# Prompt attention on one core: a head's score products in one run, then its value products

## The reference

```
o_c = softmax(q   . ck^T / 8, causal over 32 compressed blocks) . cv
o_s = softmax(q_r . ks^T / 8, causal) . vs
o_w = softmax(q_r . kw^T / 8, causal) . vw
o   = gate0 * o_c + gate1 * o_s + gate2 * o_w
```

## Time and profile before

| | us |
|---|---|
| median of 3 runs | 2354.88 |
| the profiled execution | 2356.08 |
| its span, first to last instruction | 2354.3 |
| TensorE busy with matmuls | 2059.4 (87%) |
| VectorE, ScalarE, POOL busy | 924.4, 610.2, 133.2 |
| mean granted TensorE clock | 0.838 |

### The profile page before, as it was taken

One profiled execution on the slowest core, in us unless ns is written; L12 is line 12 of the kernel. 1 busy time (PEld: TensorE's weight loads), 2 busy tenths in 40 slices (PEclk: granted clock), 3 DMA queues, 4 the chain that ended last, 5 costly groups with the idle time before them and its releaser, 6 DMA issues.

```text
span 2354.3 us, 33541 instructions
## 1 busy us (share of the span) xinstructions
PE 2059.4 (87%) x13375; PEld 1838.6 (78%) x13375; DVE 924.4 (39%) x1372; ACT 610.2 (26%) x847; POOL 133.2 (6%) x171
## 2 busy tenths in 40 slices
PE   3999676999999696997687779999998699999968
PEld 3777375999999696996574447777788699999958
DVE  4687745433334644114011122322333634343363
ACT  4222144322312223221101111222123423232223
POOL 0000003000000000004000021011100200000000
PEclk8999797999999898996666655555589799999979
DMA  4211013322222121213221200000003122222211
GB/s 131 59 36 36 18 54 118 97 83 89 89 89 89 36 77 53 72 54 92 55 62 46 72 0 1 1 1 1 1 1 99 36 90 87 91 82 79 89 36 56
DMA packets 149763, 138.82 MB, mean 59 GB/s; under 512 B 22674, under 2 KB 146914, under 8 KB 149471
## 3 DMA queue, kind: packets, MB, share of 16 engines
q1 hardware_dynamic: 148175, 129.94, 17.8%
q0 software_dynamic: 1504, 7.74, 1.0%
HBM read 130.79 MB, written 10.87 MB: 60 GB/s over the span
## 4 chain that ended last, share of the span: by engine, by line
PE 82%; DVE 9%; issue 2%; ACT 2%; SPq 1%; POOL 1%; DMA 0%; ACTq 0%; DVEq 0%; POOLq 0%
PE ps L360 47%; PE ps L1209 5%; PE ps L439 3%; PE ps L1182 3%; PE ps L399 3%; PE ps L1180 2%; PE ps L1196 2%; PE ps L1194 2%; PE ps L913 1%; DVE sub_out L1899 1%; PE ps L1052 1%; PE ps L739 1%; PE ps L738 1%; PE ps L740 1%; DVE rstd L466 1%
## 5 line engine op out<-in xcount | busy, mean ns | idle before, releaser
L360 PE MATMUL ps<-x_hi,w_hi 128*128 128x272 f32 x1920 | 409.4, 295 | 75.7 <-DVE x_lo L481 33.9
L360 PE MATMUL ps<-x_hi,w_lo 128*128 128x272 f32 x1920 | 404.1, 293 | 0.0
L360 PE MATMUL ps<-x_lo,w_hi 128*128 128x272 f32 x1920 | 403.2, 292 | 0.0
L360 PEld LDWEIGHTS ps<-x_hi,w_hi 128*128 128x128 f32 x1920 | 308.4, 193 | 84.4 <-issue 47.8
L345 DVE TENSOR_TENSOR w_lo<-w_raw,w_hi 128x2048 fp32r<-128x2048 f32 x102 | 233.6, 2293 | 250.1 <-ACT w_hi L340 249.1
L360 PEld LDWEIGHTS ps<-x_lo,w_hi 128*128 128x128 f32 x1920 | 309.3, 193 | 0.0
L360 PEld LDWEIGHTS ps<-x_hi,w_lo 128*128 128x128 f32 x1920 | 307.0, 193 | 0.0
L340 ACT ACTIVATE w_hi<-w_raw 128x2048 fp32r<-128x2048 f32 x102 | 194.5, 1907 | 296.5 <-PE ps L360 287.6
L360 PE MATMUL ps<-hid_hi,w_lo 128*128 128x272 f32 x1024 | 212.0, 288 | 0.0
L360 PE MATMUL ps<-hid_hi,w_hi 128*128 128x272 f32 x1024 | 211.6, 288 | 0.0
L360 PE MATMUL ps<-hid_lo,w_hi 128*128 128x272 f32 x1024 | 211.1, 288 | 0.0
(11 more groups left out here) (339 smaller groups left out, 2838.9 us busy)
## 6 DMA issues: line engine op xcount, KB each, us to landing
w_raw<-in_ffn_w_in SPq DMA_DIRECT2D x64, 512.0 KB, 4.6
w_raw<-in_ffn_w_out SPq DMA_DIRECT2D x64, 512.0 KB, 4.3
w_raw<-in_nsa_w_in SPq DMA_DIRECT2D x20, 512.0 KB, 4.3
w_raw<-in_conv_w_in SPq DMA_DIRECT2D x16, 512.0 KB, 5.5
w_raw<-in_ple_w_gate SPq DMA_DIRECT2D x16, 512.0 KB, 4.2
w_raw<-in_conv_w_out SPq DMA_DIRECT2D x8, 512.0 KB, 4.4
w_raw<-in_nsa_w_o SPq DMA_DIRECT2D x8, 512.0 KB, 4.6
x_tok<-in_x_prompt SPq DMA_DIRECT2D x4, 512.0 KB, 8.1
```

The lines of the kernel that those rows point to most:

```text
L360: m = pe.matmul(o_, w[par][:, wcols:wcols + P], x[:, k, c_], start=f, stop=l)
```

## The change

TensorE's step i now makes the row scores of head i + 1 and the transposed scores of head i, fill by fill in turn, with nothing between them; then, of the same head i, ten value products of the selected branch, the shift transposes, and the ten of the window branch. The compressed branch and the output transposes stand between scores and values. The loop is one step shorter, PT has one head instead of two. In a tile the correction product comes second and the mask last, and the correction of `score_rows` has 68 rows too, for which POOL clears the four rows of QB ahead of each head. ScalarE's and VectorE's lists follow. POOL's first keys, queries (of two heads now), compressed values and values are made before `end_phase` 8, behind its work for the samples, with a wait for the stores of the caches, since the buffer of the values (VX) now lies over part of their source; ScalarE's rounded copies for them stand at the start of its work for the samples.

```diff
-        (PT,), e = over(xt_at, ("pT", [P, 2, 5, SEQ], F32))
+        (PT,), e = over(xt_at, ("pT", [P, 5, SEQ], F32))
...
+        (VX,), e = over(kv_at, ("v_one", [P, 2, 2, QT, HD + 1], F32))
+        assert e <= kv_at + size([P, 2, NTT, 256]), e - kv_at
...
         def samp_act(act, L):
+            keys_high(act, L, 0)
+            for i in range(2):
+                q_high(act, L, i)
...
-        STEPS = range(-1, NHD + 1)
+        STEPS = range(-1, NHD)
...
                     pe.matmul(out, qa[:, qs], KA[g % 2][:, br, 0:n], start=True, stop=False)
-                    pe.matmul(out[:, qt * P:n], IDB[:, :], CAUB[:, :], start=False, stop=False)
-                    m = pe.matmul(out, qb[0:HD, qs], KB[g % 2][0:HD, br, 0:n], start=False, stop=True)
+                    pe.matmul(out, qb[0:HD + 4, qs], KB[g % 2][0:HD + 4, br, 0:n], start=False, stop=False)
+                    m = pe.matmul(out[:, qt * P:n], IDB[:, :], CAUB[:, :], start=False, stop=True)
                 m.then_inc(S["s_full"], 1)
...
                     pe.matmul(out, KA[g % 2][:, br, ks], qa[:, kt * P:SEQ], start=True, stop=False)
-                    pe.matmul(out[:, 0:P], CAUB[:, :], IDB[:, :], start=False, stop=False)
-                    m = pe.matmul(out, KB[g % 2][0:HD + 4, br, ks], qb[0:HD + 4, kt * P:SEQ], start=False, stop=True)
+                    pe.matmul(out, KB[g % 2][0:HD + 4, br, ks], qb[0:HD + 4, kt * P:SEQ], start=False, stop=False)
+                    m = pe.matmul(out[:, 0:P], CAUB[:, :], IDB[:, :], start=False, stop=True)
                 m.then_inc(S["t_full"], 1)
 
-            def values(i, br, j):
+            def values(i, br):
                 g = i // GQ
-                if j == 0:
-                    pe.wait_ge(S["t_exp"], 5 * i + (3, 5)[br])
-                    if i:
-                        pe.wait_ge(S[("a_free", "b_free")[br]], i)
-                    if i % GQ == 0:
-                        pe.wait_ge(S["v_prep"], 2 * (g + 1))
-                for qt, kt in V_ORDER[2 * j:2 * j + 2]:
+                pe.wait_ge(S["t_exp"], 5 * i + (3, 5)[br])
+                if i:
+                    pe.wait_ge(S[("a_free", "b_free")[br]], i)
+                if i % GQ == 0:
+                    pe.wait_ge(S["v_prep"], 2 * (g + 1))
+                for qt, kt in V_ORDER:
                     slot, c = p_tile(br, kt, qt)
-                    m = pe.matmul(PS[:, 4 + br, qt * (HD + 1):(qt + 1) * (HD + 1)], PT[:, i % 2, slot, c:c + P],
+                    m = pe.matmul(PS[:, 4 + br, qt * (HD + 1):(qt + 1) * (HD + 1)], PT[:, slot, c:c + P],
                                   VX[:, g % 2, br, kt, :], start=kt == 0, stop=kt == qt)
-                if j == 4:
-                    m.then_inc(S[("a_full", "b_full")[br]], 1)
...
                 for j in range(5):
                     if i + 1 < NHD:
                         score_rows(i + 1, j)
-                    if i >= 1:
-                        values(i - 1, 0, j)
+                    if i >= 0:
+                        score_cols(i, j)
+                if i % 2 == 0 and i >= 2:
+                    out_rows(i // 2 - 1)
                 if (i + 1) % GQ == 0 and i + 1 < NHD:
                     cmp_scores((i + 1) // GQ)
-                if i % GQ == 0 and 0 <= i < NHD:
+                if i % GQ == 0:
                     cmp_probs(i // GQ)
-                for j in range(5):
-                    if 0 <= i < NHD:
-                        score_cols(i, j)
-                    if i >= 1:
-                        values(i - 1, 1, j)
-                    if j == 2 and i + 1 < NHD:
-                        shift(i + 1)
-                if i % GQ == 0 and 0 <= i < NHD:
+                if i >= 0:
+                    values(i, 0)
+                if i + 1 < NHD:
+                    shift(i + 1)
+                if i % GQ == 0:
                     cmp_out(i // GQ)
-                if i % 2 and i >= 3:
-                    out_rows((i - 3) // 2)
+                if i >= 0:
+                    values(i, 1)
...
             def exps(i, j):
                 act.wait_ge(S["t_full"], 5 * i + j + 1)
-                if i >= 2 and j == 0:
-                    act.wait_ge(S["b_full"], i - 1)
-                L(act.activation(PT[:, i % 2, j, :], PS[:, 2 + (5 * i + j) % 2, :], ACT.Exp), S["t_exp"], wait=False)
+                if i and j == 0:
+                    act.wait_ge(S["b_full"], i)
+                L(act.activation(PT[:, j, :], PS[:, 2 + (5 * i + j) % 2, :], ACT.Exp), S["t_exp"], wait=False)
...
-                if i + 2 < NHD:
-                    q_high(i + 2)
-                if i % GQ == 0 and 0 <= i < NHD:
+                    keys_high(act, L, i // GQ + 1)
+                if 2 <= i + 2 < NHD:
+                    q_high(act, L, i + 2)
+                for j in range(5):
+                    if i >= 0:
+                        exps(i, j)
+                if i % 2 == 0 and i >= 2:
+                    out_rows(i // 2 - 1)
+                if i % GQ == 0:
                     cmp_probs(i // GQ)
-                for j in range(5):
-                    if 0 <= i < NHD:
-                        exps(i, j)
-                    if j == 2 and i + 1 < NHD:
-                        shift_rows(i + 1)
+                if i + 1 < NHD:
+                    shift_rows(i + 1)
+                if i % GQ == 0:
+                    cmp_out(i // GQ)
                 if (i + 1) % GQ == 0 and i + 1 < NHD:
                     cmp_exp((i + 1) // GQ)
...
-                if i >= 2:
-                    combine_win(i - 2)
-                if i % GQ == 0 and 0 <= i < NHD:
-                    cmp_norm(i // GQ)
+                if i >= 1:
+                    combine_win(i - 1)
                 if i + 1 < NHD:
                     for j in range(5):
                         maxima(i + 1, j)
                     shift(i + 1)
                 if (i + 1) % GQ == 0 and i + 1 < NHD:
                     cmp_max((i + 1) // GQ)
-                if i >= 1:
-                    combine_sel(i - 1)
+                if i >= 0:
+                    combine_sel(i)
+                if (i + 1) % GQ == 0 and i + 1 < NHD:
+                    cmp_norm((i + 1) // GQ)
             combine_win(NHD - 1)
...
+            L(pool.memset(QB[i % 3][HD:HD + 4, :].bitcast(F32), 0.0))
+            L(pool.tensor_copy(QA[i % 3][other, :], hi), S["q_prep"])
+            L(pool.tensor_tensor(QB[i % 3][0:HD, :], QR[rows, i // 2, 0:SEQ], hi, ALU.subtract), S["q_prep"])
...
+            keys(pool, L, 0)
+            queries(pool, L, 0)
+            queries(pool, L, 1)
+            cmp_vals(pool, L, 0)
+            pool.wait_ge(stores, 16 * N_KV_ST)
+            L(pool.memset(VX[:, :, :, :, HD:HD + 1], 1.0))
+            vals(pool, L, 0)
+
...
             samp_pool(pool, L)
+            prompt_prep(pool, L)
             end_phase(pool, 8)
```

More of the change, by code:

```diff
@@ L244, in trunk @@
         (ON, OU), _ = over(p_at, ("o_tok", [P, 2, QT, P], F32), ("o_win", [P, QT, HD], F32))
-        (OCS, PPC, PCT, VX, ATS, MXT, NMB_), e = over(
+        (OCS, PPC, PCT, ATS, MXT, NMB_), e = over(
             t_at, ("o_cmp", [P, QT, GQ, HD], F32), ("p_c", [P, QT, GQ, 32], F32), ("p_cT", [P, SEQ], F32),
-            ("v_one", [P, 2, 2, QT, HD + 1], F32), ("att_small", [P, 96], F32), ("max_cols", [P, 2, QT, 4], F32),
+            ("att_small", [P, 96], F32), ("max_cols", [P, 2, QT, 4], F32),
             ("max_bf", [P, 8], BF16))
         assert e <= t_at + 6 * 2176, e - t_at
+        (VX,), e = over(kv_at, ("v_one", [P, 2, 2, QT, HD + 1], F32))
+        assert e <= kv_at + size([P, 2, NTT, 256]), e - kv_at
         (YTOK,), e = over(f_at, ("y_tok", [P, NTT, D], F32))
@@ L1058, in samp_pe, with keys_high, q_high @@
                 pe.wait_ge(S["ots_ready"], t + 1)
+        def keys_high(act, L, g):
+            if g >= 2:
+                act.wait_ge(S["t_full"], 5 * GQ * (g - 1))
+            for br in range(2):
+                L(act.activation(KA[g % 2][0:HD, br, :], KT[:, br, g, :], ACT.Copy), S["k_hi"], wait=False)
+        def q_high(act, L, i):
+            if i >= 3:
+                act.wait_ge(S["t_full"], 5 * (i - 2))
+            rows = slice(i % 2 * HD, i % 2 * HD + HD)
+            L(act.activation(QA[i % 3][rows, :], QR[rows, i // 2, 0:SEQ], ACT.Copy), S["q_hi"], wait=False)
         def samp_act(act, L):
+            keys_high(act, L, 0)
+            for i in range(2):
+                q_high(act, L, i)
             for t in range(4):
@@ L1144, in bank_uses @@
             for i in STEPS:
+                if i % 2 == 0 and i >= 2:
+                    m1["out", i // 2 - 1] = len(m1)
                 if (i + 1) % GQ == 0 and i + 1 < NHD:
                     m1["scores", (i + 1) // GQ] = len(m1)
-                if i % GQ == 0 and 0 <= i < NHD:
+                if i % GQ == 0:
                     m1["probs", i // GQ] = len(m1)
@@ L1150, in bank_uses @@
                     m0["shift", i + 1] = len(m0)
-                if i % GQ == 0 and 0 <= i < NHD:
```

(30 more changed lines are left out.)

63 lines of the change are left out of this document (10 added, 53 removed).

## The result

The changed kernel takes 2211.65 us (median of 4 runs, 2208.89 to 2213.72), the one before 2355.11 beside it (4 runs, 2352.86 to 2372.43). The ratio is 0.9365, interval 0.9324 to 0.9405. Forecast were 2191 us and a range of 2165 to 2290. The profiled execution took 2208.89 us: span 2207.1, mean granted clock 0.885 (before 0.838).

The account below looks back on a forecast made before the run. TensorE, mostly at half clock, was taken to bound the prompt attention. Its terms summed to 228.1 us plus 11.4 of waits, 239.5 against 404.4, so 164.9 less than 2356.1: 2191 us, range 2165 to 2290.

Parts of the forecast that it names:

- The start, -12.4 us: Start of prompt attention: POOL's preparation moves under the sample attention, so TensorE starts 12.4 us earlier.
- Row tiles at the transposed tiles' price: TensorE's row scores: with 68 rows a row tile costs what a transposed one does, 2.7 us less a head.
- Masks last, nothing: Score tiles: putting the mask's product last in each tile was priced at nothing.
- The steps: TensorE's loop: a new step takes 11.86 us at the high level against 14.49, plus 0.3 us of waits.
- The level: TensorE's clock: rises at the latest in the first head's step, then stays high; 10.5 us a step, chance 0.55.
- Waits: New waits in the loop: 4.8 us over the steps and 6.6 at group starts, 11.4 together.
- The row tiles keep their price: Rival on row tiles: order or side, not 64 rows, makes their price; +44 us, 2235 us, chance 0.10.
- The level comes and goes: Rival on TensorE's clock: 4 to 11 of the 15 steps low, 2233 to 2307 us, chance 0.28.
- Its neighbour in the Trainium skill: Rival on TensorE's clock: a new order gains no clock, about ten steps low, 2294 us; no chance of its own.
- Slower: Rival: the compressed-branch run no longer raises the level; all steps low, with waits in each head 2386 us, chance 0.02.

Follow-up runs that it names:

- e3: Kernel before, only with 68 instead of 64 rows in the row tiles' correction product and POOL's clearing; 2224.20 us, ratio 0.9412.
- e1: Changed kernel with the row tiles' correction product back at 64 rows; 2289.76 us, ratio 0.9687.
- e12: e7 with 64 rows again in the row tiles' correction product; 2350.17 us (2304.46 to 2355.86), no ratio.
- e7: Kernel before with 68 rows, POOL's preparation ahead of `end_phase` 8, compressed scores two steps and normalization one step earlier; 2179.59 us, ratio 0.9234.
- e9: e6 with 64 rows again in the row tiles' correction product; 2227.48 us, ratio 0.9428.
- e6: Changed kernel with each group's compressed scores two steps and its normalization one step earlier; 2193.55 us, ratio 0.9281.
- e8: e6 with output transposes at the end of a step and the compressed output's halves swapped; 2180.17 us, ratio 0.9236.
- e5: Changed kernel with POOL's and ScalarE's preparation of the first group back behind `end_phase` 8; 2224.21 us, ratio 0.9420.
- e10: Changed kernel with 65 instead of 68 rows in the row tiles' correction product; 2211.02 us, ratio 0.9352.
- e2: Changed kernel with the mask's product second in each tile again; 2212.87 us, ratio 0.9377.
- e4: e3 with the mask last in every tile; 2217.03 us, ratio 0.9378.
- e11: e7 with the first group's compressed scores ahead of the first row tiles; 2179.37 us, ratio 0.9217.

## Why the prediction was right, and where it was not

Medians side by side, in us (early start in all but the two of the kernel before and e3, which would be 12.6 lower with it):

| | 64 rows | 68 rows |
|---|---|---|
| old order | 2354.9 | 2224.2 (e3) |
| new order | 2289.8 (e1) | 2211.7 (the change) |
| old order, early branch | 2350.2 (e12, its fastest run 2304.5) | 2179.6 (e7) |
| new order, early branch | 2227.5 (e9) | 2193.6 (e6), 2180.2 (e8) |

*The start, -12.4 us*: right. e5 gives 12.6 back; TensorE starts at 1361.93, though after an idle stretch of 2.17 us and not within 1 us of the samples' last product.

*Row tiles at the transposed tiles' price*: right, 0.60 against 0.59 us. The forecast chose this from unlike tiles; e1 and e10 show that it is the 64 rows. At the high level without drops it is e9's 34 us, 2.1 a head instead of the 2.7 taken. The Trainium skill (TensorE: Matmul & The Clock Gate, "LDWEIGHTS (loading the stationary operand)") has a load's row count make no difference to its time. Of the load itself this is so here, 0.18 us with 64 rows and 0.19 with 68. What the forecast drew from it, that the tiles then cost the same, is not (2289.8 against 2211.0 us for 64 and 65 rows): the cost is in when the load starts, not in how long it takes.

*Masks last, nothing*: right in the new order (e2); in the old one the stage is 3.0 us longer in e4's trace than in e3's, so e4's -7 us can't be credited to it.

*The steps*: right. Forecast 11.86 us and 0.3 of waits, 12.16 together; step 1 takes 1410.53 - 1398.39 = 12.14. It holds 0.3 of wait, too short for the list: its third row fill starts 0.55 us behind the tile before (1400.87 to 1401.42), in step 2 0.30. e8 has such steps at 11.82. Step 2, at 12.21 with 0.44 of output transposes, has none.

*The level*: half right, and this is the step that failed. "After it no step holds what all three drops had in common, slow row tiles with value products between them": this pair was indeed what kept the old kernel low. With the slow tiles apart (e9) and with fast tiles mixed (e7) the level stays at 1.00 through the loop once the waits are gone; with both together (e12) it does not, waits or no waits. That the value products are the half of the pair that matters is not shown: the new order also takes row and transposed fills in turn, and no run parts the two. But "so the level should stay" left out a second cause: a wait of 1 to 2 us of TensorE can be followed by 13.6 to 20.5 us at 0.50 (e3 too, 2.04 us), with 64 rows even by 133 (e1). That such waits set it off rests on e6, which removed wait and drops together, and on the other traces: in the eight kernels with 65 or 68 rows that wait at the high level for 1.14 to 2.04 us (the change, e2 to e6, e8, e10), 19 of 23 such waits have a drop during them or within 2.4 us behind, and no drop in the loop stands without one. e7 and e11 have no such wait at the high level and no drop. The same 1.80 us at 1506.24 had no drop behind it, so what decides in the single case is open. The term costs 16.0 us.

*Waits*: their sum was right by luck (12.3 against 11.4), not their places. The per-step waits (4.8) came only as the 0.3 in odd steps, and the listed ones, nearly all in the groups' first steps, were 12.3 instead of 6.6. The 7.1 on VectorE's maxima were missing. "In this stage nobody holds TensorE up but POOL" had passed over the 2.07 us at 1395.51, and I moved the normalization behind the combination in VectorE's list without asking what is late next. It is ahead of the maxima that free TensorE's banks.

The stage came out 17.4 us long: drops +16.0, listed waits +0.9 (12.3 against all 11.4), the rest +0.5. The first two steps, 1361.93 to 1398.39, took 36.5 us with their waits in place of 36.7 without. 2191 + 17.4 = 2208.4, the profiled 2208.89.

*The rivals.* "The row tiles keep their price" was put at +44 and measures +78 (e1), because a dearer tile takes the level with it. "The level comes and goes" came in part, two stretches instead of 4 to 11 steps. Its neighbour in the Trainium skill (same page, "Part 1: The HAM clock gate"), that sustained matmuls release the throttle, is not borne out: as in the 99.0 us of the earlier trace rows, e12 is busy without a gap for 102.0 us and stays at 0.50. (The ten low steps that the prediction priced there make 2296 at 10.5 us each, not 2294.) "Slower" is off: all three long rises came right behind the compressed output, with a wait of 0.77 us ahead of it each time, and in e8 at 1397.6 without one. A short rise, at 1375.8, came 2.5 us into step 0's score tiles and was gone at 1379.2, behind a wait of 1.14 us.

*What the forecast credited to the wrong part.* It gave 10.5 us a step to the level and held the new order to be what brings it. That the total still fell into the range is partly luck: the row count, priced at 2.7 us a head, brought the level too. With 68 rows the new order brings nothing that can be measured (e7 against e8; e3 less 12.6 is 2211.6, the change 2211.7). Its worth shows at 64 rows: 2354.9 less 12.6 is 2342.3, against e1's 2289.8, 52 us, and with the early branch 2350.2 against 2227.5, or 77 us by e12's fastest run. The row count is worth 131 us in the old order and 78 in the new. The two gains do not add, as would follow if each removes the same pair.

## What to carry to other kernels

Where TensorE is busy all the time and still reads 0.50, look for a product whose shape makes its neighbours slow, in this case one of 64 rows whose weight load starts no earlier than the product itself, and try it one row larger before the order of the queue is rewritten. When two edits land together, run each alone: here two lines, the row count and POOL's clearing, gave 131 of 143 us. Once the level is high, a short wait can cost more than its length, so look in the list of the engine that frees TensorE's buffers for work that can be done a step earlier.

## What was not expected of the hardware

- A 64-row product among 128-row ones costs a tile of 384 columns 0.27 us at the high level (0.76 against 0.49). Its load takes 0.18 us but starts with its product; one of 65 or 68 rows takes 0.19 and starts 0.05 to 0.24 ahead in the new order.
- Busy without a gap is not enough for 1.00: 100 and 102 us at 0.50 in e12, 133.1 in e1 at 98% busy; 5% idle in the changed kernel (96.81 busy of 102.40) did not lower it.
- Value products cost 4.63/40 = 0.116 us an instruction at the high level and, from 1386.67 to 1390.83, 4.16/20 = 0.208 at the low.
